# Spreading the inverse of the 32x32 blocks over eight steps a piece, and its mask in another buffer

## The reference

```python
pc = project(hc, w_in[i])                       # context tokens, 256
oc, ctx_states = deltanet(pc, lp, 1, CTX_LEN, (zero, zero))
hx = rmsnorm(x, norm_g[i]) * (1.0 + sc_x) + sh_x
px = project(hx, w_in[i])                       # 2048 tokens: q k v z_a beta a hy z_b g_a g_b
ox, _ = deltanet(px, lp, rows, GRID_W, ctx_states)
yx = hyena(px, lp, rows, GRID_W)
x = x + gt_x * merge(px, ox, yx, lp)

def chunk_gated_delta(q, k, v, g, beta, s0):    # inside deltanet, cut
    decay = jnp.exp(jnp.where(incl, gc[..., :, None] - gc[..., None, :], -jnp.inf))
    lmat = jnp.where(strict, jnp.einsum('nbhid,nbhjd->nbhij', kb, kc) * decay, 0.0)
    a_sys = lmat + jnp.eye(CHUNK, dtype=lmat.dtype)
    sol = lax.linalg.triangular_solve(a_sys, rhs, left_side=True, lower=True, unit_diagonal=True)
```

## Time and profile before

| | us |
|---|---|
| three runs | 4481.42, 4488.98, 4489.99 (median 4488.98) |
| the profiled execution | 4487.66 |
| its span | 4485.6 |
| PE busy in the span | 4236.8 (94%) |
| DVE busy in the span | 2429.5 (54%) |
| projections, first to last step | about 137 to 2345 |

### The profile page before, as it was taken

One profiled execution on the slowest core, in us unless ns is written; L12 is line 12 of the kernel. 1 busy time (PEld: TensorE's weight loads), 2 busy tenths in 40 slices (PEclk: granted clock), 3 DMA queues, 4 the chain that ended last, 5 costly groups with the idle time before them and its releaser, 6 DMA issues. The chain is left out here.

```text
span 4485.6 us, 72316 instructions
## 1 busy us (share of the span) xinstructions
PE 4236.8 (94%) x28915; PEld 2586.8 (58%) x28915; DVE 2429.5 (54%) x3482; ACT 1231.5 (27%) x2590; POOL 1766.7 (39%) x1487
## 2 busy tenths in 40 slices
PE   5899999999999999999988999989999986999998
PEld 3466544444445544444436888856565654767775
DVE  4555855442456778987215666657676764222221
ACT  4122111111222211111114555556555551000000
POOL 1222223333233343333329999945444452111111
PEclk7999999999999999999998999999999997999999
DMA  6323222233243334244228888657777677223320
GB/s 227 105 74 101 71 98 77 80 103 107 80 159 93 99 113 117 71 118 125 103 91 213 217 250 256 190 156 223 227 215 211 206 249 279 85 75 105 120 75 28
DMA packets 481065, 627.05 MB, mean 140 GB/s; under 512 B 120929, under 2 KB 379945, under 8 KB 470125
## 3 DMA queue, kind: packets, MB, share of 16 engines
q1 hardware_dynamic: 431596, 484.22, 35.7%
q0 software_dynamic: 28560, 113.25, 7.9%
q10 hardware_dynamic: 20592, 25.16, 1.7%
HBM read 405.01 MB, written 217.53 MB: 139 GB/s over the span
## 5 line engine op out<-in xcount | busy, mean ns | idle before, releaser
L1453 PE MATMUL proj_b<-shared_S,proj_tw 128*128 128x512 f32 x1920 | 848.4, 593 | 0.0
L1453 PE MATMUL proj_b<-shared_A,shared_wt 128*128 128x512 f32 x1280 | 590.1, 605 | 38.0 <-issue 26.2
L1453 PEld LDWEIGHTS proj_b<-shared_S,proj_tw 128*128 128x128 f32 x1920 | 360.6, 190 | 432.7 <-issue 432.3
L820 POOL TENSOR_TENSOR proj_tw<-shared_wt 128x512 f32<-128x512 f32 x80 | 113.6, 1419 | 956.0 <-PE proj_b L1453 872.8
L1453 PEld LDWEIGHTS proj_b<-shared_A,shared_wt 128*128 128x128 f32 x1280 | 247.5, 194 | 352.7 <-issue 352.3
L1453 PE MATMUL proj_b<-shared_S,shared_wt 128*128 128x512 f32 x640 | 292.8, 601 | 0.0
L1453 PE MATMUL proj_b<-shared_A,proj_tw 128*128 128x512 f32 x640 | 288.1, 593 | 4.5 <-DVE proj_u L1127 4.5
L1025 ACT ACTIVATE proj_v<-proj_b 128x512 f32<-128x512 f32 x80 | 47.8, 597 | 633.0 <-PE proj_b L1453 633.0
L1835 DVE SCALAR_TENSOR_TENSOR delta_la<-delta_kkq,delta_sc,delta_wm 128x256 f32<-128x256 f32 (+1 forms) x288 | 121.7, 464 | 174.0 <-PE delta_kkq L1934 173.9
L1122 DVE TENSOR_TENSOR proj_u<-proj_b,proj_u 128x512 f32<-128x512 f32 x80 | 55.3, 691 | 296.6 <-PE proj_b L1453 296.5
L1699 POOL TENSOR_SCALAR delta_ex<-delta_rows,delta_sc 128x128 f32<-128x128 f32 x288 | 204.4, 726 | 22.3 <-DMA delta_tnc<-scratch_Tn 22.3
(11 more groups left out here) (333 smaller groups left out, 8567.1 us busy)
## 6 DMA issues: line engine op xcount, KB each, us to landing
shared_wt<-in_w_in_dram POOLq DMA_DIRECT2D x80, 1024.0 KB, 6.0
delta_nv<-scratch_NV SPq DMA_DIRECT2D x144, 256.0 KB, 4.1
delta_kq<-scratch_KQ SPq DMA_DIRECT2D x128, 256.0 KB, 4.3
scratch_bounce_f<-tail_first SPq DMA_DIRECT2D x128, 256.0 KB, 4.4
tail_yf<-scratch_bounce_f SPq DMA_DIRECT2D x32, 1024.0 KB, 7.5
scratch_bounce_i<-fft_yi SPq DMA_DIRECT2D x64, 512.0 KB, 3.4
fft_second<-scratch_bounce_i SPq DMA_DIRECT2D x32, 1024.0 KB, 8.7
scratch_hy<-proj_tok SPq DMA_DIRECT2D x48, 512.0 KB, 2.6
```

The lines of the kernel that those rows point to most:

```text
L820: pool.tensor_tensor(T3, w[:, hi, second], w[:, lo, second], ALU.subtract).then_inc(combined, 1)
L1453: last = pe.matmul(bank[:, :], weights[:, k, :], aa[operand][:, k, :], start=(k == 0), stop=(k == KH - 1))
```

## The change

A piece of the inverse takes eight steps in place of six, so that the pieces start at steps 53, 61 and 69 (before: 53, 59, 65).

- n = 0: as before.
- n = 1: times KK in slot 0, the first direction's scaling in slot 2, and in slot 4 the second direction's scaling (it becomes setup part 2).
- n = 2: masking and diagonal (now part 3) in slot 1; rounds 1, 2 in slot 2, 3, 4 in slot 3, 5, 6 in slot 4.
- n = 3 to 6: six rounds a step, 7 to 30: one in each of slots 0 to 3, two in slot 4. The turn stands in slot 4 of n = 6.
- n = 7: nothing.

The inverse loads are issued in steps 52, 60, 68, the stores in 59, 67, 75 (before: 57, 63, 69). `low` is a view of `hc` and its load waits for the first product of step 40 in place of the last read of the old x2; gate loads no longer wait for the masking. In `invert_setup(i, n)` of the diff, n is the part of the setup: 1 the forward scaling, 2 the backward scaling, 3 the mask.

```diff
--- before.py
+++ after.py
@@ -560,7 +560,7 @@
 NBK = 2 * NCH * H * NSB // P
 NPIECE = 3
 PB = NBK // NPIECE
-PIECE_STEPS = 6
+PIECE_STEPS = 8
 PRODUCTS = ("P1", "P6", "P7", "P5", "P2", "P4", "P3")
 
 
@@ -688,7 +688,7 @@
         nw = [kit.sb("nw1", FE, FW), kit.sb("nw2", FW, FW), kit.sb("nw3", FW, FW)]
         nbias, nfreq = kit.sb("nbias", FW, 3), kit.sb("nfreq", FW, 1)
 
-        low = x2[:, 0, :, :].rearrange("p g c -> p (g c)")
+        low = hc[:, 0:SB * SB // CTX, :].rearrange("p k t -> p (k t)")
         dtb, alog = kit.sb("dtb", P, 2 * H), kit.sb("alog", P, 2 * H)
         GN = NCH * 4 * H
         e, t1, t3, sg = (region[:, GN * i:GN * (i + 1)].rearrange("p (c r) -> p c r", r=4 * H) for i in range(4))
@@ -896,7 +896,6 @@
                     elif h:
                         old = first_step(0, "zb") + KT // 2 - 1
                         sp.wait_ge(side_read["dve"], read_count["turn", old, m, len(groups_of(old)) - 1])
-                        sp.wait_ge(istep, 2 * (4 + 2 * (SB - 2)) + 4)
                     sp.wait_ge(tok_out[m], 16 * tok_dmas[s - KT // 2 + 1])
                     sp.dma_start(x2[:, m, :, :], split_rows(T["hy"][2 * KT + b + m], h)).then_inc(gate_in[m], 16)
 
@@ -908,8 +907,7 @@
                         sp.wait_ge(net_out, 64)
                         sp.wait_ge(sc_out, 48)
                         sp.wait_ge(g_out, 16)
-                        old = first_step(0, "zb") + KT // 2 - 1
-                        sp.wait_ge(side_read["dve"], read_count["turn", old, 0, len(groups_of(old)) - 1])
+                        multiplied_by(sp, first_step(1, "q"), "P1")
                         sp.dma_start(low[:, :], T["low"].broadcast_to([P, SB * SB])).then_inc(gc_in, 16)
                         for d in range(2):
                             sp.dma_start(gcv[halves[d], :, :], flat(T["gcT"][d])).then_inc(gc_in, 16)
@@ -1215,6 +1213,11 @@
                 flat = lambda t: t.rearrange("p n j i -> p n (j i)")
                 whole = lambda t: t.rearrange("p n j i -> p (n j i)")
                 ROUNDS = SB - 2
+                ROUNDS_AT = {(2, 2): (1, 2), (2, 3): (3, 4), (2, 4): (5, 6)}
+                for n in range(3, 7):
+                    for slot in range(5):
+                        first = 7 + 6 * (n - 3) + slot
+                        ROUNDS_AT[n, slot] = (first,) if slot < 4 else (first, first + 1)
                 ISTEPS = 4 + 2 * ROUNDS
 
                 def invert_spread(i):
@@ -1240,8 +1243,9 @@
                         dve.wait_ge(beta_in, 32)
                         dve.wait_ge(istep, base + 1)
                         dve.tensor_tensor(eb[forth], eb[forth], by_col(bv[forth, mine, :]), ALU.mult)
+                    if n == 2:
                         dve.tensor_tensor(eb[back], eb[back], by_row(bv[back, mine, :]), ALU.mult).then_inc(istep, 1)
-                    if n == 2:
+                    if n == 3:
                         dve.wait_ge(istep, base + 2)
                         dve.tensor_tensor(flat(nb), flat(eb), low[:, :].unsqueeze(1).broadcast_to([P, PB, SB * SB]), ALU.mult).then_inc(istep, 1)
                         dve.wait_ge(istep, base + 3)
@@ -1267,12 +1271,13 @@
                         return
                     if n == 0 and slot == 1:
                         invert_spread(i)
-                    if n == 1 and 1 <= slot <= 3:
-                        invert_setup(i, slot - 1)
-                    if 2 <= n <= 4:
-                        for k in range(1 + 10 * (n - 2) + 2 * slot, 3 + 10 * (n - 2) + 2 * slot):
-                            invert_round(i, k)
-                    if n == 4 and slot == 4:
+                    if n == 1 and slot in (0, 2, 4):
+                        invert_setup(i, slot // 2)
+                    if n == 2 and slot == 1:
+                        invert_setup(i, 3)
+                    for k in ROUNDS_AT.get((n, slot), ()):
+                        invert_round(i, k)
+                    if n == 6 and slot == 4:
                         invert_turn(i)
 
                 done = [0]
```

## The result

The changed kernel took **4445.69 us** (median of four runs, 4442.41 to 4451.92) against 4489.48 us for the kernel before (four runs). The ratio is 0.9913, with a 95% interval of 0.9900 to 0.9926. The profiled execution took 4446.54 us, its span is 4444.8 us, 40.8 less than before. The prediction said 4446.

What follows compares the result with a forecast made beforehand. PE was taken to wait on DVE's issue order ahead of C11 in steps 53 to 69, losing 45.38 us; step 53 keeps 3.59, saving 41.8: 4487.66 - 41.8 = 4445.9, say 4446 us, range 4436 to 4461.

Steps and rivals of the forecast that it cites:

- The rival that the gaps are not DVE's: PE's gaps in the inverse's steps would stay, 4488 us; chance 3%.
- The deadline: C11 on DVE must start by about t = 21.6 in a 25.80 us step, 20.7 in a 24.92 one.
- the replay: DVE's order slot by slot: C11 at t = 20.5 in step 65, slack 1.1; 19.5 in step 57, slack 1.2.
- Part 1, step 53: Spread (n=0) unchanged: step 53 keeps its loss of 3.59 us; steps 61 and 69 lose nothing.
- Parts 2 and 3: Setup and masking (n=1, n=2) spread over slots: losses of 8.13, 7.25 and 2.68 go; C11 by 19.2 and 19.
- Part 4: Six rounds a step, n=3 to 5: n=4 full at 25.8 to 27.1 us; losses of 4.40, 8.96, 8.55 go.
- The rival that used up the slack: More held instructions ahead of C11 in steps 57, 58, 65, 66: 4450 to 4461 us; chance 10%.
- The slower rival: Nearly all rounds run beside POOL in steps 57, 58, 59, 64 to 67: 4526 us; chance 4%.
- Part 5, the turn: Turn of 5.42 us in slot 4 of n=6: C12 at t = 26.1, some 7 us before its product.
- Part 6, steps 71 to 76: These steps now hold DVE rounds of 6 to 11 us, which fit before C11: cost 0.
- part 8: SP's queue: piece 1's store moves to step 67, piece 2's load to 68; cost 0, bounds 0 to 3.
- Part 7, the mask: Mask moves from x2 to hc; the new wait is long past and gate loads lose one: cost 0.

Runs made afterwards that it cites:

- Experiments 1 and 2: 1: changed kernel with the setup where it stood before, 4459.86 us; 2: changed kernel with ten rounds a step in n=3 to 5, 4459.82 us.
- experiment 4: Changed kernel plus extra 704-element products on DVE in slot 3, one in step 57, three in step 65: 4442.9 us (one run).
- experiment 3: Kernel before with only the mask moved from x2 to hc and its waits changed: 4487.31 us against 4486.89, ratio 0.9999.
- experiment 9: The changed kernel run again unedited, on another occasion: 4444.99 us.
- last store later: Changed kernel with the last piece stored in step 76's turn of SyncE's list in place of step 75's: 4442.2 us (one run).

## Why the prediction was right, point by point

- *What bounds.* The 45.38 us of losses were DVE's order ahead of C11. Experiments 1 and 2 brought back 14.8 and 17.7 us in the steps named for each part, and nowhere else. The rival that the gaps are not DVE's is out. Together they bring back 32.4 of the 41.8 that the steps behind 53 had lost. What they leave out is the place of the third piece: its steps lost 16.3 us before (66, 67, 68), and only 3.3 in the two experiments (70, 73), where next to nothing is convolved. The prediction didn't name this share. The numbers don't add up exactly, as steps 54 and 57 lost more in the experiments than before (4.26 and 7.46 against 2.68 and 4.40).
- *The deadline* of t = 21.6 measures 21.5 (experiment 4), and the 0.78 us from C11 to PE held in every gap read (0.78, 0.79). The least margin, 0.3 us in step 61, stood outside the replay: "took 25.80" in step 59 says that a step is in time, not by how much.
- *Part 1, step 53.* The mechanism held; the size was off. The term of 3.59 measured 5.03, and 3.5 to 7.3 over eight executions with an unchanged spread. Its cause was left at "as before" because one execution of the kernel before was all there was; the row beside it, 3.70 us for the products after a gap of 3.33, was taken for the rule, although step 60 showed the clock falling after a gap of 5.32, and step 57 after one of 2.02, shorter than that of step 53 (last section).
- *Parts 2 and 3.* Steps 54, 55, 62, 63, 70 and 71 lose nothing, as said. C11 of step 62 starts at t = 19.04 (19.2 at the latest was said), that of step 63 at 19.70 (19 at most was said).
- *Part 4.* Called full but not late: true. DVE is busy 22.66, 23.56 and 24.77 us in steps 64, 65 and 66, where 25 was expected; the replay came within 0.3 us (it had three round instructions held and C22 free, the trace two and C22). The sum beside it, 25.8 us for step n=4, was 2.2 too high for step 65. It took over 4.2 us of held instructions from step 62, where step 65 has 3.0 (two rounds and C22). Where the other 1.0 went is not resolved. The rival that used up the slack did not come. By the rule of the Trainium skill ("SBUF — State Buffer", "Who interferes with whom") the step would have been held for all of POOL's 8.9 us; the trace disagrees with that reading, not with the rule: U3, with one input from a bank, ran beside POOL's first sum and was no longer for it (0.69 us, as long as U2 of the same step, which ran with POOL idle), while C22, with two inputs from SBUF, went to 1.75, and of POOL's 8.9 us in step 65 some 1.9 show in the rounds and 1.1 in C22; the taps' part is there in calm steps too. The slower rival, built on all twelve held, fell with two of twelve held in step 65.
- *Part 5, the turn:* C12 of step 67 starts at 2006.04, 25.9 us after its mark, as late as expected; nobody waits, and step 68 takes 25.80.
- *Part 6, steps 71 to 76.* DVE's work cost nothing there, but step 76 lost 0.90 through part 8.
- *Part 7, the mask.* 0, measured by itself (experiment 3).
- *Part 8, SP's queue.* For piece 1 it held: the load of piece 2 is issued at t = 20.6 of step 68, where 20 was said, and costs nothing. For the last piece this step failed. Cost 0 was argued with piece 1, behind whose stores stand token stores and a gate load with a step's slack. For the last piece only the landing before the end was looked at. Before the change its store stood in step 69, where no channel store follows; in step 75 the channel store of step 74 follows, and C22 waits for that. What was missing is the list of what is queued behind the moved wait at its new place, which the za, ga, gb steps would have given. It measured 0.90 us, within the bounds of 0 to 3, though these were argued for piece 1.
- *The sum.* 41.8 expected, 39.45 from the steps: 1.44 less from step 53, 0.90 from step 76. The time came out at 4446 because the stages ahead and behind happened to be 1.4 us shorter, the execution is longer than its span by 0.3 us less, and the median of the changed kernel lies 0.85 below its profiled execution. The exact agreement is luck; the size of the saving is not. The clock's price in two of the rivals, "up to 2.9" from step 60, is 8.13 - 5.32 = 2.81; experiment 9 paid 3.03 over its gap.

## What to carry to other kernels

Work that fills a second engine's idle time is free only up to the instruction that the first engine waits for next: find that instruction, replay the order of issue up to it in the fullest step and in every step that holds one long instruction ahead of it, and put long work behind it instead of ahead of it. When a store is moved in a queue, list what stands behind it at the new place, and who waits for that, for every instance of a loop and not for one. Before a long step is called late, compare PE's busy time with its length.

## What the runs showed of the hardware

The price of one and the same gap differs between executions, and between steps of one execution. Gap before the products, the time the eight products behind it took (3.67 or 3.70 at full speed), and what the step lost, all in us:

| kernel, step | gap | products | loss |
|---|---|---|---|
| before, 53 | 3.33 | 3.70 | 3.59 |
| last store later, 53 | 3.27 | 3.70 | 3.53 |
| mask alone, 53 | 3.30 | 5.35 | 5.21 |
| ten rounds, 53 | 3.36 | 5.24 | 5.15 |
| changed kernel, 53 | 3.17 | 5.31 | 5.03 |
| extra products, 53 | 3.97 | 5.16 | 5.68 |
| before, 54 | 2.45 | 3.67 | 2.68 |
| setup as before, 54 | 2.45 | 5.26 | 4.26 |
| setup as before, 53 | 1.87 | 5.40 | 3.82 |
| setup as before, 70 | 1.88 | 3.67 | 2.11 |
| before, 57 | 2.02 | 5.37 | 4.40 |
| changed kernel again, 53 | 4.31 | 6.47 | 7.34 |
| before, 60 | 5.32 | 6.23 | 8.13 |
| before, 66 | 5.32 | 5.37 | 7.25 |

The rows of steps 57 and 66 of the kernel before, which the prediction doesn't show:

```profile
1749.93 5.37 PE L1453 MATMUL proj_b<-shared_A,shared_wt 128*128 128x512 f32 x8 [2.02 <-issue]
...
2006.98 5.37 PE L1453 MATMUL proj_b<-shared_A,shared_wt 128*128 128x512 f32 x8 [5.32 <-issue]
```

After gaps of 1.9 to 3.4 us the products ran at full speed in some rows and partly at 1.2 GHz in others, 1.5 to 1.7 us dearer (granted clock 1.00 in step 53 of the kernel before, 0.94 in its step 57 and in step 53 of the changed kernel). In the kernel before alone, 2.02 us of gap had this price and 3.33 us did not, so the length of the gap does not decide it in this range; what does is not shown. The Trainium skill, "TensorE: Matmul & The Clock Gate", section "What's actually happening", says of the clock's rise at the start of a kernel that it comes at another point from run to run; the rows show the same of its fall within a kernel. A saving of gaps has this term on top. One profile can show that it varies, as this one did in its steps 53 and 57, but not its size for one step.
